# A weight ring of six half tiles in place of three whole tiles, in a kernel that chains six transformer blocks

## What is computed

```python
STAGES = [("s5",), ("moe", 0), ("sb",), ("moe", 1), ("conv", 0), ("ffn", 0), ("lru",), ("ffn", 1),
          ("mla",), ("ffn", 2), ("conv", 1), ("ffn", 3)]
```

```python
def grouped_moe(x, router_w, router_bias, w1, w3, w2):
    ...
    h = jax.nn.silu(jnp.einsum('td,edf->etf', xt, w1)) * jnp.einsum('td,edf->etf', xt, w3)
    h = h * gates.T[:, :, None].astype(h.dtype)
    y = jnp.einsum('etf,efd->td', h, w2)

def swiglu_ffn(xn, w_gu, w_down):
    gate, up = jnp.split(xn @ w_gu, 2, axis=-1)
    return (jax.nn.silu(gate) * up) @ w_down
```

## Time and profile before

| | us |
|---|---|
| median of 3 runs | 2556.77 |
| lowest and highest | 2556.48, 2556.78 |
| the profiled execution | 2551.28 |
| its span | 2549.5 |
| mean granted TensorE clock in it | 0.944 of full speed |

### The profile page before, as it was taken

One profiled execution on the slowest core, in us unless ns is written; L12 is line 12 of the kernel. 1 busy time (PEld: TensorE's weight loads), 2 busy tenths in 40 slices (PEclk: granted clock), 3 DMA queues, 4 the chain that ended last, 5 costly groups with the idle time before them and its releaser, 6 DMA issues.

```text
span 2549.5 us, 27439 instructions
## 1 busy us (share of the span) xinstructions
PE 2263.8 (89%) x11242; PEld 1894.0 (74%) x11242; DVE 1545.8 (61%) x1661; ACT 1129.4 (44%) x1066; POOL 40.0 (2%) x41
## 2 busy tenths in 40 slices
PE   5479999888898999988799999679995799999999
PEld 4357887666877888776598888668884578889887
DVE  7975557777545555777775446755456654556554
ACT  3124445555353444556445344544443353443543
POOL 1220000000000000000000000000000000000000
PEclk9688999999898999999899999889997899999999
DMA  6022557778421355778645454325541045545453
GB/s 237 17 83 103 195 198 283 293 300 310 150 83 67 137 193 214 294 297 301 230 165 182 182 191 152 136 108 189 184 180 66 34 149 188 192 152 192 179 188 116
DMA packets 62811, 453.05 MB, mean 178 GB/s; under 512 B 7104, under 2 KB 7104, under 8 KB 7904
## 3 DMA queue, kind: packets, MB, share of 16 engines
q1 hardware_dynamic: 61344, 443.57, 47.4%
q0 software_dynamic: 1056, 6.95, 0.7%
q10 hardware_dynamic: 288, 0.80, 0.1%
HBM read 450.24 MB, written 1.05 MB: 177 GB/s over the span
## 4 chain that ended last, share of the span: by engine, by line
PE 69%; DVE 15%; ACT 7%; DMA 4%; issue 4%; POOL 1%; SPq 0%; ACTq 0%; DVEq 0%; POOLq 0%
PE bank L296 17%; PE bank L298 16%; PE bank L297 16%; DVE w_lo L276 6%; ACT w_hi L267 5%; DMA raw<-in_stream 4%; PE bank L289 4%; PE bank L290 3%; PE bank L291 3%; PE bank L861 1%; DVE scr L2248 1%; PE bank L580 1%; DVE scr L2232 1%; PE bank L853 1%; DVE c_lo L1150 1%
## 5 line engine op out<-in xcount | busy, mean ns | idle before, releaser
L276 DVE TENSOR_TENSOR w_lo<-raw,w_hi 128x2048 fp32r<-128x2048 f32 x421 | 965.1, 2293 | 771.1 <-ACT w_hi L267 770.7
L267 ACT ACTIVATE w_hi<-raw 128x2048 fp32r<-128x2048 f32 x421 | 806.1, 1915 | 969.7 <-PE bank L298 740.2
L296 PE MATMUL bank<-w_hi,x_hi 128*128 128x512 f32 x1024 | 405.0, 396 | 4.0 <-DVE x_lo L491 4.0
L298 PE MATMUL bank<-w_hi,x_lo 128*128 128x512 f32 x1024 | 400.9, 392 | 0.0
L297 PE MATMUL bank<-w_lo,x_hi 128*128 128x512 f32 x1024 | 400.7, 391 | 0.0
L296 PE MATMUL bank<-w_hi,c_hi 128*128 128x512 f32 x872 | 343.7, 394 | 44.7 <-issue 21.9
L298 PE MATMUL bank<-w_hi,c_lo 128*128 128x512 f32 x872 | 341.7, 392 | 0.0
L297 PE MATMUL bank<-w_lo,c_hi 128*128 128x512 f32 x872 | 341.4, 392 | 0.0
L289 PE MATMUL bank<-x_hi,w_hi 128*128 128x256 f32 x792 | 229.7, 290 | 28.0 <-DVE w_lo L276 23.3
L290 PE MATMUL bank<-x_lo,w_hi 128*128 128x256 f32 x792 | 228.3, 288 | 0.0
L291 PE MATMUL bank<-x_hi,w_lo 128*128 128x256 f32 x792 | 228.0, 288 | 0.0
(11 more groups left out here) (391 smaller groups left out, 2263.4 us busy)
## 6 DMA issues: line engine op xcount, KB each, us to landing
raw<-in_stream SPq DMA_DIRECT2D x421, 1024.0 KB, 4.8
ln_rows<-in_ln POOLq DMA_DIRECT2D x4, 1024.0 KB, 5.0
scr<-in_xt SPq DMA_DIRECT2D x1, 1024.0 KB, 5.3
scr<-in_s POOLq DMA_DIRECT2D x1, 1024.0 KB, 14.8
x<-in_x POOLq DMA_DIRECT2D x1, 1024.0 KB, 20.1
out_x<-x SPq DMA_DIRECT2D x4, 256.0 KB, 2.6
par<-in_par ACTq DMA_DIRECT2D x1, 752.5 KB, 10.6
scr<-in_ple POOLq DMA_DIRECT2D x1, 512.0 KB, 10.7
```

The costliest lines, as they stand in the source:

```text
L267: nc.scalar.activation(w_hi[:, n % RING, :], raw[:, n % RING, :], ACT.Copy).then_inc(hi_done, 1)
L276: nc.vector.tensor_tensor(w_lo[:, n % RING, :], raw[:, n % RING, :], w_hi[:, n % RING, :].bitcast(F32), ALU.subtract).then_inc(lo_done, 1)
L296: nc.tensor.matmul(out, xh, hi, start=start, stop=False)
L298: return nc.tensor.matmul(out, xl, hi, start=False, stop=stop)
```

## The change

A tile is now 8 blocks, 512 KB, 4 KB in each partition, and the ring has six of them, so that the memory stays the same. A call of `split_hi` or `split_lo` at an old place now does two half tiles one after the other, each with its own waits and its own signal. SP issues 840 transfers of 512 KB in place of 421 of 1 MB: the `s5` and `lru` stages need 19 and 33 half tiles where 10 and 17 whole ones stood. PE waits and releases by half tiles. Its matmuls are the same in kind and number; in `up`, `down`, `ple_pe` and `outer_pe` they run in another order, since both token tiles now go over each half tile before the next. The lead at a stage's end is 4 half tiles (`LEAD`). Some signals share a semaphore ("start hi", "start lo", "raw"). The diff, cut to its core; the ffn's `up` changes as the experts' does:

```diff
@@ -20,18 +20,19 @@
 KC = D // P
 TT = T // P
 HALF = D // 2
-BLOCKS_PER_TILE = 16
+BLOCKS_PER_TILE = 8
 SLAB = 4
 SLABS_PER_TILE = BLOCKS_PER_TILE // SLAB
 TILE = BLOCKS_PER_TILE * P
-RING = 3
+RING = 6
+LEAD = 4
 N_EXPERTS = 16
 GROUPS = 4
 SLOT_TILES = 5
 SLOTS = SLOT_TILES * P
 REST = SLOTS - T
-EXPERT_TILES = 6
-MOE_LEAD = 5
+EXPERT_TILES = 12
+MOE_FIRST = 10
 D_EXPERT = 512
 D_FF = 2816
 UNIT = 4 * P
...
@@ -254,27 +255,26 @@
         act_at, dve_at, pe_at = Stream(), Stream(), Stream()
 
 
-        def split_hi(act):
-
-            n = act_at.tile
-            if n == n_tiles:
-                return
-            act_at.tile += 1
-            act.wait_ge(raw_in[n % RING], 16 * (n // RING + 1))
-            if n >= RING:
-                used, count = pe_did.tile(n - RING)
-                act.wait_ge(used, count)
-            nc.scalar.activation(w_hi[:, n % RING, :], raw[:, n % RING, :], ACT.Copy).then_inc(hi_done, 1)
-
-        def split_lo(dve):
-
-            n = dve_at.tile
-            if n == n_tiles:
-                return
-            dve_at.tile += 1
-            dve.wait_ge(hi_done, n + 1)
-            nc.vector.tensor_tensor(w_lo[:, n % RING, :], raw[:, n % RING, :],
-                                    w_hi[:, n % RING, :].bitcast(F32), ALU.subtract).then_inc(lo_done, 1)
+        def split_hi(act, tiles=2):
+
+            for n in range(act_at.tile, min(act_at.tile + tiles, n_tiles)):
+                act.wait_ge(raw_in[n % RING], 16 * (n // RING + 1))
+                if n >= RING:
+                    used, count = pe_did.tile(n - RING)
+                    act.wait_ge(used, count)
+                nc.scalar.activation(w_hi[:, n % RING, :], raw[:, n % RING, :], ACT.Copy).then_inc(hi_done, 1)
+                act_at.tile = n + 1
+
+        def split_lo(dve, tiles=2):
+
+            for n in range(dve_at.tile, min(dve_at.tile + tiles, n_tiles)):
+                dve.wait_ge(hi_done, n + 1)
+                nc.vector.tensor_tensor(w_lo[:, n % RING, :], raw[:, n % RING, :],
+                                        w_hi[:, n % RING, :].bitcast(F32), ALU.subtract).then_inc(lo_done, 1)
+                dve_at.tile = n + 1
+
+        def lead_of(st):
+            return (starts + [n_tiles])[st] + LEAD
 
         def block_of(t, b):
             s = slice(b * P, (b + 1) * P)
...
@@ -584,20 +585,19 @@
                     after(H3[j], ("dve", ("h_lo", st, u, j)))
 
             def down(u, part):
-                n = take_tile()
                 chunks_ = widths[u] // P
-                pe.wait_ge(dve_did["h_lo"], dve_did.at("h_lo", st, u, part))
-                for tt in range(TT):
-                    for j in range(2):
-                        c = 2 * part + j
+                for c in (2 * part, 2 * part + 1):
+                    n = take_tile()
+                    pe.wait_ge(dve_did["h_lo"], dve_did.at("h_lo", st, u, part))
+                    for tt in range(TT):
                         for half in range(2):
                             b = Y[2 * tt + half]
                             if u == 0:
                                 before(pe, b)
                             final = u == last_unit and c == chunks_ - 1
                             mm = three_by_token(b[:, :], h_hi[:, c, tokens(tt)], h_lo[:, c, tokens(tt)],
-                                                slab_of(n, SLAB * (2 * j + half)), u == 0 and c == 0, final)
-                            end = tt == TT - 1 and j == 1 and half == 1
+                                                slab_of(n, SLAB * half), u == 0 and c == 0, final)
+                            end = tt == TT - 1 and half == 1
                             if final:
                                 mm.then_inc(pe_did["y"], pe_did.next("y", st, tt, half, tile=n if end else None))
                             elif end:
...
@@ -978,23 +973,24 @@
 
             def up(u, part, banks, label):
                 pos, e, visits = UNITS[u]
-                n = take_tile()
-                for tt in range(visits):
-                    if part == 0:
-                        before(pe, banks[tt])
-                    for j in range(SLABS_PER_TILE):
-                        k = SLABS_PER_TILE * part + j
-                        if u == 0 and tt == 0 and label == "h1" and k % 2 == 0:
-                            pe.wait_ge(dve_did["xg_lo"], dve_did.at("xg_lo", st, k // 2))
-                        if u == 4 and label == "h1":
-                            pe.wait_ge(dve_did["xg_lo"], dve_did.at("xg_lo", st, 4 + k))
-                        xh, xl = input_of(pos, tt, k)
-                        mm = three_by_token(banks[tt][:, :], xh, xl, slab_of(n, SLAB * j), k == 0, k == KC - 1)
-                    tile = n if tt == visits - 1 else None
-                    if part == 1:
-                        mm.then_inc(pe_did[label], pe_did.next(label, st, u, tt, tile=tile))
-                    elif tile is not None:
-                        mm.then_inc(pe_did["tile"], pe_did.next("tile", tile=tile))
+                for first in (4 * part, 4 * part + 2):
+                    n = take_tile()
+                    for tt in range(visits):
+                        if first == 0:
+                            before(pe, banks[tt])
+                        for j in range(SLABS_PER_TILE):
+                            k = first + j
+                            if u == 0 and tt == 0 and label == "h1" and k % 2 == 0:
+                                pe.wait_ge(dve_did["xg_lo"], dve_did.at("xg_lo", st, k // 2))
+                            if u == 4 and label == "h1":
+                                pe.wait_ge(dve_did["xg_lo"], dve_did.at("xg_lo", st, 4 + k))
+                            xh, xl = input_of(pos, tt, k)
+                            mm = three_by_token(banks[tt][:, :], xh, xl, slab_of(n, SLAB * j), k == 0, k == KC - 1)
+                        tile = n if tt == visits - 1 else None
+                        if k == KC - 1:
+                            mm.then_inc(pe_did[label], pe_did.next(label, st, u, tt, tile=tile))
+                        elif tile is not None:
+                            mm.then_inc(pe_did["tile"], pe_did.next("tile", tile=tile))
 
             def turn_h(u):
                 visits = UNITS[u][2]
...
@@ -1012,22 +1008,23 @@
 
             def down(u, half):
                 pos, e, visits = UNITS[u]
-                n = take_tile()
-                for j in range(visits):
-                    pe.wait_ge(dve_did["h_lo"], dve_did.at("h_lo", st, u, j))
-                for tt in range(visits):
-                    b = y_bank(pos, tt, half)
-                    if e == 0:
-                        before(pe, b)
-                    for c in range(4):
-                        mm = three_by_token(b[:, :], h_hi[:, c, tokens(tt)], h_lo[:, c, tokens(tt)], slab_of(n, SLAB * c),
-                                            e == 0 and c == 0, e == 3 and c == 3)
-                    tile = n if tt == visits - 1 else None
-                    if e == 3:
-                        mm.then_inc(pe_did["expert y"], pe_did.next("expert y", st, pos, tt, half, tile=tile))
-                        after(b, ("dve", ("y_lo", st, pos, tt, half)))
-                    elif tile is not None:
-                        mm.then_inc(pe_did["tile"], pe_did.next("tile", tile=tile))
+                for first in (0, 2):
+                    n = take_tile()
+                    if first == 0 or visits == TT:
+                        pe.wait_ge(dve_did["h_lo"], dve_did.at("h_lo", st, u, first // 2))
+                    for tt in range(visits):
+                        b = y_bank(pos, tt, half)
+                        if e == 0 and first == 0:
+                            before(pe, b)
+                        for c in (first, first + 1):
+                            mm = three_by_token(b[:, :], h_hi[:, c, tokens(tt)], h_lo[:, c, tokens(tt)], slab_of(n, SLAB * (c - first)),
+                                                e == 0 and c == 0, e == 3 and c == 3)
+                        tile = n if tt == visits - 1 else None
+                        if e == 3 and first == 2:
+                            mm.then_inc(pe_did["expert y"], pe_did.next("expert y", st, pos, tt, half, tile=tile))
+                            after(b, ("dve", ("y_lo", st, pos, tt, half)))
+                        elif tile is not None:
+                            mm.then_inc(pe_did["tile"], pe_did.next("tile", tile=tile))
 
             def scatter(pos, half):
                 parts = range(TT if pos == 0 else 1)
...
@@ -737,25 +732,25 @@
 
         def ple_pe(pe, st):
             li = stages[st][1]
-            n = starts[st]
-            assert pe_at.block == n * BLOCKS_PER_TILE
-            pe_at.block += BLOCKS_PER_TILE
-            pe.wait_ge(lo_done, n + 1)
-            pe.wait_ge(dve_did["p_lo"], dve_did.at("p_lo"))
-            for tt in range(TT):
-                for half in range(2):
```

(20 more changed lines are left out.)

## The result

The changed kernel takes 2457.85 us, median of four runs (2455.46 to 2457.98); the kernel before, beside it, 2556.62 (2552.53 to 2556.78). The ratio is 0.9611, with a 95% interval of 0.9599 to 0.9623. The profiled execution took 2457.98 with a span of 2456.2, against 2551.28 and 2549.5 before.

What follows compares the result with a forecast made beforehand. PE's program sets the time, so only its waits and half-clock stretches can be won. Experts 62, stage ends 9.4, mixers 11, less 2, is 80 us off 2551.3: 2471, with 5.5 for the median 2477; range 2464 to 2515.

Steps and rivals of the forecast that it cites:

- What bounds the kernel, and the loop: Expert units with one token tile: a closed loop of whole-tile handoffs takes 20.2 us, with PE busy for 17.22.
- Transfers: Transfers of half tiles: 3.5 us to land, from 4.8 for 1 MB and 2.6 for 256 KB; ends 2.6 and 4.8.
- The loop in half tiles: Expert units: the handoff loop shrinks to 15.1 us and a second one to 16.2, both below PE's own 17.2.
- imperfect fit: Expert units: 0.3 us a unit left as not gained, 6 us of 58.
- What that gives: Both expert stages: 52 us in the twenty units, 2.8 in the units before them, 7.4 in the last: 62.
- Ends of stages and mixers: Outside the experts: 9.4 us from earlier last splits at stage ends, 11 from shorter handoffs in the mixers.
- Waits and releases: Whole kernel: PE's 419 more waits and as many more signals cost nothing.
- longer pairs: Mixers where DVE is the bound: two half splits take 2.35 us for 2.29, costing 1 to 2 us in all.
- The offset: Whole kernel: the median of the runs lies 5.5 us above the profiled execution, so 2471 becomes 2477.
- R1: Rival, chance 0.2: transfers set the expert unit at 18.4 us instead of 17.5; 2499 us in all.
- R2: Rival, chance 0.06: a transfer's fixed part is partly serial, 0.44 us each; units of 22.9 us, slower at 2597.
- R3: Rival, chance 0.12: another order in the hand-placed calls binds at about 19 us a unit, half the experts' gain; 2508.

Runs made afterwards that it cites:

- e3: Kernel before with only the splits of ACT and DVE in halves, transfers and releases whole: 2503.33 us, ratio 0.9791.
- e5b: Changed kernel, but ACT splits a half tile only when PE has done with both halves of the former pair: 2483.39 us, ratio 0.9712.
- e4b: Changed kernel, but SP issues when both halves of a pair are free and ACT waits until both have landed: 2486.48 us, ratio 0.9716.
- e1: Kernel before with each 1 MB transfer issued as two of 512 KB, ACT waiting for both: 2583.61 us, ratio 1.0106.
- e7b: Changed kernel with the rounding of h and its low part between the two halves of a pair in the expert units: 2448.1 us, ratio 0.9569.
- e2: Kernel before with each 1 MB transfer issued as four of 256 KB, ACT waiting for all: 2625.63 us in a single run.
- e8: Changed kernel with the last two splits of lru held until PE has used its last half tile there: 2462.75 us, ratio 0.9623.
- e6b: Changed kernel with the last two splits of lru held until PE is 1.4 us before its end there: 2464.61 us, ratio 0.9637.

## Why the prediction was too high

The mechanism held; the sum was too small. Three steps of it failed. A wait of PE outside the experts was priced by its idle time alone, with nothing for the half clock: that fell by 19 us there, and 2.5 us in ffn1 are shown to come from it. The edges of the expert stages had no term and gave 5.1 us. And 5.5 us were added for an offset that the changed kernel does not have. What the rest of the 6.9 us outside the experts comes from stays open in part.

**What bounds the kernel, and the loop: right.** The ten units lost their waits, the chain went from handoffs to matmuls (PE 78% of it, 69% before), and e3, e5b and e4b show that the granularity of the splits, of the releases and of the transfers carries it. The fall to PE's own program, 17.2 a unit, came to 17.4 to 18.1.

**Transfers: mis-sized.** The line through 1 MB and a write of 256 KB gave 3.5 us for a half tile. The medians, by how many were under way at the issue (four more had five):

```
under way at the issue   0     1     2     3     4
transfers              115   376   131   117    97
us to land             3.2   4.2   4.6   5.4   5.6
```

The 3.5 is thus near for a lone one. The Trainium skill, DMA: Bandwidth & Descriptors, section Anatomy of one DMA, has a fit that gives 3.2, an estimate. It is a fit for transfers issued by GpSimd, and these are issued by SyncE; the trace agrees for those 115 alone. With the finer ring up to five are under way, and in the units the median is 5.4 (the one on the chain above 5.58). Transfers of 1 MB took 4.8 with none or one under way, so no row of before gave a warning. The rule of the Trainium skill to batch transfers to at least 1 MB, in section Bandwidth of the same page, is about the share of the peak, and its table too was measured with GpSimd issuing. In e1 the trace agrees that halves are dearer, 334 GB/s when full for 377. In the changed kernel 336 GB/s at a share of 0.91 would be 369 when full, a little less than 377 as well, but the time went down: there the rule does not decide.

**The loop in half tiles: wrong in length, without harm to the sum.** 15.1 us was forecast with 3.03 on PE. The chain needs 17.9 from the release at 502.43 to PE's start at 520.30, where the forecast had 12.1 for the same way. Of the 5.8 us between them 2.1 are the transfer (5.58 for 3.5), and 3.4 low parts: four stand in a row ahead of the gate, 4.63 us, not one of 1.22. It nearly fits only because this way begins where PE wants the w3 tiles of one unit and ends where it wants those of the next, and 17.1 us of matmuls lie between the two. This is why 0.3 us a unit were left, taken as imperfect fit, and measured 0.4 (183.1 and 181.8 against the 178.5 and 178.3 of e7b).

**What that gives: 62 forecast, 68.4 measured.** The twenty units gave 53.9 for 52, the units ahead 3.3 for 2.8, the last ones 6.1 for 7.4. The 5.1 us at the edges of the stages had no term: the first unit behind the routing and the way to the last y. And PE's floor is 178.4, not the 180.2 that the typical unit of the earlier trace rows gave.

**Ends of stages and mixers: 20.4 forecast less 2, 24.9 measured.** By stage, forecast and measured: s5 5.2 and 7.3, sb 1.6 and 2.6 (which is within sb's own scatter), lru 9.0 and 7.7, mla 3.9 and 2.3, conv1 0.9 and 2.3, the ffn stages and conv0 nothing and 2.9 (2.5 of it behind lru). At the end of s5 PE still waits for the last x, where the earlier trace rows had 3.7:

```profile
PE bank L296 <- DVE x L452: 1.0, 1, 1.0
```

At the end of lru the wait is gone, as forecast. The start of s5 gave 2.4 us, not 1.1: the first low part begins at 19.50 instead of 20.88:

```profile
19.50 4.78 DVE L272 TENSOR_TENSOR w_lo<-raw,w_hi 128x1024 fp32r<-128x1024 f32 x4
```

DVE's work ahead of it is the same; it depends on the parameters, which landed after 9.2 us instead of 10.6. In e1, e2 and e3, with whole tiles, they landed after 9.4 to 10.3, and PE still began at 22.7 to 23.5, against 20.8 to 21.0 in each kernel with half tiles. So not all of it is chance; why they land earlier was not tried.

**The clock outside the experts: the term that was left out.** The prediction read the half-clock time as part of the excess of the experts, and priced every wait elsewhere by its idle time alone. It fell by 19 us elsewhere (lru 6.9, ffn1 6.8, s5 3.4, conv1 3.4, sb 2.0, and mla 3.4 more). The parts of s5 and sb are no larger than what they vary by between runs of the changed kernel (64.9 to 68.3 and 11.1 to 17.1 us); lru, ffn1, mla and conv1 had the same half-clock time in all three of its traces. In ffn1, where PE works all the time, 6.8, 7.9 and 9.5 us at half clock (before, e8, e3) made the stage 2.5, 2.8 and 3.5 us longer. The 2.5 are what e8 brought back by a wait of 4.3 us. In the other stages, where PE also idles at half clock, its share was not taken apart.

**Waits and releases: nothing, as forecast;** the ffn stages, with PE busy throughout, kept their 189 to 190 us with twice the waits. The 2 us taken off for longer pairs are not to be seen either.

**The offset.** 5.5 us were added for the median of the runs over the profiled execution. For the changed kernel the two are equal (2457.85 and 2457.98). The offset belonged to one execution of before, not to the kernel. So of the 19 us of the miss 5.5 are this, 6.4 the experts (68.4 for 62), and 6.9 the rest of the trace (24.9 for the 18 that 80 leaves).

**The rivals.** R1 was partly there: ACT waits 14.6 us for transfers in the first ten units, and they land in over 5, but PE sees 7 of it at most, and with e7b's order nothing. R2's price is real (e1, e2), though its sum has a slip (20.2 less six times 2.9 is 2.8, not 2.6), and it lies off the path. R3's idea, another order that still binds, is what e7b shows, at 0.4 us a unit instead of 2. A range down to 2464 held only residuals of the loop, the transfers and the mixers. Without the offset of 5.5 and with the 2.5 of ffn1 its low end would have been 2456, just below the 2457.85 measured.

## What to carry over

When single full engines explain nothing and the chain of waits closes on itself, count the handoffs and halve what is handed on; but halve splits, releases and transfers together, since transfers cut alone made this kernel slower by 1.1%. Take a transfer's time for the number that will be under way, not for a lone one, and price a wait of PE with the half clock that follows it, also outside the stretch that is changed. Afterwards look at what stands between two halves of a pair: moving one rounding there gave 8 us more in the expert units, and the same in lru, mla and the second conv another 7.5.

## What the runs showed of the hardware

- A transfer of 512 KB lands 3.2 us after its issue when alone and 5.6 with four under way. One of 1 MB takes 4.8 with none or one under way. Cut in two it takes 5.6 from the first issue in the ten units of e1, in four 6.9 (e2).
- SP takes 0.33 us for a further issue of the same tile, on the chain of e1.
- At 345 GB/s and a DMA share of 0.93 to 0.94 (e7b) PE did not wait for transfers.
- At a wait of 2.9 us of PE ahead of the ffn stage the granted clock stayed at 2.4 GHz in e6b's profiled execution and fell in e3; at 3.7 (before, e1) and 4.3 us (e8) it fell, and that stage had 6.8, 8.6 and 7.9 us at half clock. So the length of the wait alone does not decide.
- The longer the waits, the more busy time for the same matmuls: 178 us in e7b's ten units, 184 before, 192 in e1, 197 in e2, at clocks of 1.00, 0.98, 0.93 and 0.90.
